# Paged decode steps moved between the steps of a stick-breaking attention sweep

## The reference

```python
def block(inp):                       # prompt, 128 queries at a time
    z = jnp.einsum('bqhd,bshd->bhqs', qi, kf) * Dh ** -0.5 + bias
    mask = kpos[None, :] < pi[:, None]
    l1mb = jnp.where(mask, jax.nn.log_sigmoid(-z), 0.0)
    after = lax.cumsum(l1mb, axis=3, reverse=True) - l1mb
    A = jnp.where(mask, jnp.exp(jax.nn.log_sigmoid(z) + after), 0.0)
    return jnp.einsum('bhqs,bshd->bqhd', A, vf)
```

## Time and profile before

| what | value |
|---|---|
| time, median of 3 runs | 1577.14 us (1576.19 to 1581.95) |
| the profiled execution | 1576.19 us, span 1574.2 us |
| PE busy | 1292.1 us (82% of the span) |
| DVE, ACT, POOL busy | 844.5, 485.1, 357.4 us |
| mean granted clock of PE | 0.897 |
| stage of the change | about 151 to 560 us of the span |

### The profile page before, as it was taken

How to read it: one execution, slowest core, us unless ns; L and a number is a source line. 1 busy time by engine, 2 the same in 40 slices (tenths; PEclk the granted TensorE clock), 3 DMA queues, 4 the chain that set the end, 5 groups by cost and what they waited for, 6 DMA issues and landing times. The chain is left out here.

```text
span 1574.2 us, 23116 instructions
## 1 busy us (share of the span) xinstructions
PE 1292.1 (82%) x7719; PEld 1082.3 (69%) x7719; DVE 844.5 (54%) x1198; ACT 485.1 (31%) x902; POOL 357.4 (23%) x235
## 2 busy tenths in 40 slices
PE   3549599799798855878969789499999998697997
PEld 2449467677576545878968789478787886365885
DVE  4434789889795613847668387244444443323221
ACT  5312345345355512141331413231313131222110
POOL 0027544343340002536334264000000000000000
PEclk7679789899898987999989999698999898798998
DMA  4536657477382505464444642285656541543320
GB/s 134 161 115 205 208 178 243 136 223 234 124 249 74 181 23 183 135 195 135 141 130 129 198 143 83 92 252 166 188 164 187 165 148 70 176 151 112 107 80 28
DMA packets 200420, 237.89 MB, mean 151 GB/s; under 512 B 13539, under 2 KB 122434, under 8 KB 200298
## 3 DMA queue, kind: packets, MB, share of 16 engines
q1 hardware_dynamic: 196338, 224.61, 46.2%
q0 software_dynamic: 3968, 11.87, 2.1%
HBM read 215.88 MB, written 20.64 MB: 150 GB/s over the span
## 5 line engine op out<-in xcount | busy, mean ns | idle before, releaser
L248 PE MATMUL bank<-xh,b_w_hi 128*128 128x344 f32 x480 | 167.0, 348 | 57.4 <-ACT b_mix L257 17.5
L1961 POOL TENSOR_TENSOR cp_keys<-cp_keys,cp_q 128x1024 f32<-128x1024 f32 x64 | 161.0, 2533 | 159.0 <-DMA cp_keys<-cache_sb_k 158.9
L1961 POOL TENSOR_TENSOR bp_keys<-bp_keys,bp_q 128x1024 f32<-128x1024 f32 x64 | 156.8, 2470 | 177.0 <-DMA bp_keys<-cache_sb_k 169.2
L248 PE MATMUL bank<-xl,b_w_hi 128*128 128x344 f32 x480 | 162.5, 339 | 0.0
L248 PE MATMUL bank<-xh,b_w_lo 128*128 128x344 f32 x480 | 162.4, 338 | 0.0
L248 PE MATMUL bank<-xh,d_w_hi 128*128 128x344 f32 x384 | 131.4, 342 | 24.2 <-DVE d_w_lo L231 16.5
L317 PE MATMUL bank<-xh,c_w_hi 128*128 128x344 f32 x384 | 130.3, 339 | 17.0 <-DVE c_w_lo L303 17.0
L248 PEld LDWEIGHTS bank<-xh,b_w_hi 128*128 128x128 f32 x480 | 98.6, 205 | 61.8 <-ACT b_w_hi L226 24.0
L317 PE MATMUL bank<-xl,c_w_hi 128*128 128x344 f32 x384 | 127.1, 331 | 0.0
L317 PE MATMUL bank<-xh,c_w_lo 128*128 128x344 f32 x384 | 126.7, 330 | 0.0
L248 PE MATMUL bank<-xl,d_w_hi 128*128 128x344 f32 x384 | 126.5, 329 | 0.0
(11 more groups left out here) (381 smaller groups left out, 2587.9 us busy)
## 6 DMA issues: line engine op xcount, KB each, us to landing
cp_keys<-cache_sb_k SPq DMA_DIRECT2D x128, 256.0 KB, 3.0
cp_values<-cache_sb_v SPq DMA_DIRECT2D x128, 256.0 KB, 3.0
bp_keys<-cache_sb_k SPq DMA_DIRECT2D x128, 256.0 KB, 3.1
dp_values<-cache_sb_v SPq DMA_DIRECT2D x128, 256.0 KB, 2.8
b_w_raw<-w_in SPq DMA_DIRECT2D x20, 512.0 KB, 4.0
c_w_raw<-w_in SPq DMA_DIRECT2D x16, 512.0 KB, 5.3
d_w_raw<-w_in SPq DMA_DIRECT2D x16, 512.0 KB, 5.1
o_mix<-mix SPq DMA_DIRECT2D x8, 1024.0 KB, 5.7
```

The lines of the kernel that those rows point to most:

```text
L248: last = self.nc.tensor.matmul(self.bank(j, c)[:, 0:self.width], w[:, s, k, :], x[:, k, c * self.width:(c + 1) * self.width], start=(k == ...
L1961: self.nc.gpsimd.tensor_tensor(self.keys[:, s], self.keys[:, s], q, ALU.mult).then_inc(self.scaled.sem, 1)
```

## The change

The paged parts are put at other steps. Taking and gathering the sum of the sample before goes to the very top of step 0 on both engines, and keeping it to the end of step 0. The page sums and the exponents go from step 2 to step 1, ACT's exponential from step 3 to step 2. The eight groups of paged weighings stood in steps 4 to 11 and now stand in steps 3 to 6 and 8 to 11.

```diff
-    GROUPS = (4, 5, 6, 7, 8, 9, 10, 11)
+    GROUPS = (3, 4, 5, 6, 8, 9, 10, 11)
...
@@ block.scalar
-                if u == 3 and i < GT:
+                if u == 2 and i < GT:
                     load_tables(nc, act, LN_EXP)
                     act.wait_ge(values.weighed.sem, values.weighed.at(i, 0))
                     keys.weights(act, i)
...
@@ block.vector
                 i, u = g // NU, g % NU
+                if u == 0 and i:
+                    values.take_partial(dve, i - 1)
                 if u == V_TURNED + 1:
...
                 if u == 0 and i:
-                    values.take_partial(dve, i - 1)
-                if u == 1 and i:
                     values.keep(dve, i - 1)
-                if u == 2 and i < GT:
+                if u == 1 and i < GT:
                     keys.exponents(dve, i)
...
@@ block.tensor
                 i, u = g // NU, g % NU
+                if u == 0 and i:
+                    values.gather(pe, i - 1)
                 if g < LAST:
                     scores(g)
                 if g in chunk_of:
                     stream.chunk(pe, *chunk_of[g][1:])
-                if u == 1 and i:
-                    values.gather(pe, i - 1)
-                if u == 2 and i < GT:
+                if u == 1 and i < GT:
                     if i:
                         pe.wait_ge(values.kept.sem, values.kept.at(i, 0))
                     keys.sum_pages(pe, i)
```

## The result

| | before | after |
|---|---|---|
| median (range, runs) | 1577.22 us (1576.19 to 1581.95, 4) | 1596.87 us (1591.54 to 1603.41, 4) |
| ratio after/before | | 1.012, 95% interval 1.0078 to 1.0164 |
| profiled execution, its span | 1576.19, 1574.2 us | 1599.24, 1597.2 us |
| stage of the change | 460.8 us | 474.3 us |
| mLSTM stage, two stages on | 405.5 us | 413.2 us |

The changed kernel is slower, and its median lies 0.9 us above the upper end of the range. The stage times are the distances between barriers; the stages not named moved by 1.2 us at most.

The account below looks back on a forecast made before the run. PE was taken as the bound (busy 89% of sweep 1), with stage changes entering the span one for one. Terms 3.2 + 4.4 + 3.0 + 6.4 - 3.0 - 3.0 + 1.0 = +12.0 us gave 1588 us, range 1576 to 1596.

Parts of the forecast that it names:

- boundary 0/1, wait, gather, clock: From sweep 0 to 1, PE waits 3.2 us for the masked copy ahead of the gather; low clock adds 3.2.
- boundary 1/2, wait, gather, clock: From sweep 1 to 2, PE waits 4.35 us for the masked copy ahead of the gather; low clock adds 3.2.
- gather's time, given back: Gather moves from step 1 to step 0 on PE and costs nothing net; page sums take its place.
- boundary 2/3, steps 11 to 2: From sweep 2 to 3, no chunk in step 0: PE starts 4.8 us later, partly an old wait; +3.0 us.
- steps 3 and 4 of sweeps 1 and 2: Exponents one step earlier free DVE ahead of the copy PE awaits in step 4: -1.5 us each, -3.0 in all.
- weighings, values: Four paged weighings one step earlier: waits for values of 0.85 and 2.71 us go; -3.0 us in sum.
- end of sweep 3: PE waits for the copy between its last weighing and the gather: +1.0 us, bounds 0 and 1.0.
- The clock: After idling at the two boundaries with a chunk, PE runs about 6.4 us at half clock: +3.2 us each, +6.4.
- the clock stays up: Rival: 3 to 4 us of idling does not lower PE's clock at two boundaries; +5.6 us, 1582 us, chance 0.15.
- It is worse: Rival: clock down as long as in sweep 3 at each boundary, POOL products hit moved scans; 1596 us, chance 0.08.
- the scan goes first: Rival: step 3's scan keeps the port ahead of POOL, saving 9.3 us in two sweeps; 1570 us, chance 0.05.
- the broken burst: Rival: POOL's four products break up, scan enters after two, saving 4.7 us in sweeps 1 and 2; 1579, chance 0.10.

Follow-up runs that it names:

- second trace: Changed kernel run again with nothing altered: 1592.64 us, ratio 1.0094; for the kernel before, likewise run again unaltered: 1578.82 us, ratio 1.0004.
- short products: GpSimd's key products over 64 of 512 columns, as a test only: 1565.87 us in the changed kernel, 1547.25 us in the kernel before.
- old groups: Changed kernel with the eight groups of paged weighings back at steps 4 to 11: 1599.44 us, ratio 1.0132.
- the kernel with the later store: Changed kernel with the gather at the end of step 0 and GpSimd's store of the gated half three key pairs later: 1562.47 us, ratio 0.9879.
- the kernel before with the later store: Kernel before with only GpSimd's store of the gated half put three key pairs later (pair 8 for 5): 1569.45 us, ratio 0.9936.

## Why the prediction was right and wrong

The direction, the cause and its place were right: a copy queued on DVE behind the softplus holds PE at every boundary. The gather alone at the top brings the loss, and the gather at the end of the step removes it. The size was off. The measured terms, from the length of the steps (the start of one step's scores to the next), both traces against the first trace of the kernel before; against its second trace the sum is 3.6 us more:

| term | forecast | first trace | second trace |
|---|---|---|---|
| boundary 0/1, wait, gather, clock | 3.2 + 3.2 | +8.4 | +8.5 |
| boundary 1/2, wait, gather, clock | 4.4 + 3.2 | +11.9 | +13.0 |
| gather's time, given back (page sums took its place in step 1, and left step 2) | 0 net | -1.7 | -1.7 |
| boundary 2/3, steps 11 to 2 | +3.0 | +0.1 | +0.4 |
| steps 3 and 4 of sweeps 1 and 2 | -3.0 | -4.7 | -4.7 |
| weighings, values | -3.0 | -5.1 | -3.0 |
| end of sweep 3 | +1.0 | +4.8 | +3.2 |
| sweep 0 and its start | 0 | -0.2 | -2.5 |
| sum | +12.0 | +13.5 | +13.1 |

**The step that failed is the size of the waits at boundaries 0/1 and 1/2.** They were forecast at 3.2 + 4.4 us and measured at 5.2 + 9.4 (second trace 6.0 + 9.6). Two things were missed.

The first is when PE arrives. The prediction took its arrival from before and only moved the copy. But that arrival held a wait for values ahead of the last weighing: 1.52 us at 0/1, and 1.0 us at 1/2. Both went with the change, apart from 0.66 us at 0/1 in the second trace. The prediction called 0.85 and 2.71 us the largest such waits in reach and passed over the 1.52 us in its own row. With short products, where POOL cannot disturb DVE for long, the wait is 4.72 us at every boundary.

The second is the queue ahead of the copy. At 1/2 the prediction asked whether the copy could be shut out by POOL, and answered with an operation that reads PSUM. That was right: at 272.03 the copy took its 0.68 us inside a product that ran from 271.79 to 274.31. It did not ask the same of the multiplications ahead of it, which read two tiles in SBUF. They lost 4.2 us, as the moved weighings brought the key products forward; the old groups and the short products both took that away.

**The clock** was priced about right, at 3.2 + 3.2 us. What the steps grew by is new idle time, the gather and the clock. PE's work in steps 11 and 0 is 14.3 us before and 15.3 us with the gather at the full clock. In the changed kernel it is 19.0 and 17.8 us (second trace 17.7 and 18.6), so the low clock costs 3.8 + 2.5 = 6.3 us (2.4 + 3.4 = 5.8). The idle time grew by 3.7 and 8.4 us, the waits less the values' waits that went, and the gather's 1.0 us each makes up the rest of +8.4 and +11.9. The rival in which the clock stays up is refuted at all three boundaries. The rival "It is worse" has the number of the first result, 1596, but not its terms: the clock was down for 10.2 us at each of the two boundaries, as in sweep 3 of before, and cost 6.3 us and not 10; and POOL's products hit the multiplications ahead of the copy, while the moved scans of the exponents took 0.2 us each.

**Boundary 2/3** was forecast at +3.0 and cost nothing. The kernel before already stood 3.33 us there and already ran at the low clock. In steps 11 to 2 PE's idle time grew only from 4.1 to 5.7 us, since most of the old wait went, and its work fell from 22.9 us (22.3 in the second trace of before) to 21.4 (21.7). The low clock there lasted 10.2 and 6.8 us before and 6.8 us in both traces after. **The end of sweep 3** was forecast at +1.0 and cost 3 to 5. The copy stood behind both multiplications of the last step (562.12 to 563.39), so the wait was 2.26 us and not 0.68, and with the low clock the transposes and the weighing behind it took nearly twice as long. The prediction applied the clock to two boundaries and left out the end.

**The savings** were real and too low: the kernel with the gather at the step's end shows them undisturbed. The waits for values nearly went, as forecast, and in sweep 3 steps 8 to 10 gained 4.7 us (4.3 in the second trace). Steps 3 and 4 took 2.0 to 2.8 us less a sweep, where 1.5 were taken; against the mean of both traces of before it is 2.0. The old groups keep this gain and the gather alone does not have it, so it belongs to the page sums, the exponents and ACT's exponential, which moved together.

**The scans** stayed shut out, 11.62 us. The Trainium skill (SBUF — State Buffer, section "SBUF: two separate sides") has the pair of ports locked for one instruction. The traces agree with that nearly everywhere: each of the two multiplications above waited for one product though the products stood back to back, and in the kernel with the later store a scan beside one product of 2.45 us took 2.52. In the mLSTM stage of before, POOL runs four products in a row, and a scan gets in behind each:

```profile
706.41 9.38 POOL L1961 TENSOR_TENSOR bp_keys<-bp_keys,bp_q 128x1024 f32<-128x1024 f32 x4 [2.60 <-DMA mix<-b_mix]
...
708.78 2.43 DVE L2009 TENSOR_TENSOR_SCAN bp_page_soft<-ones,bp_page_L 128x32 f32<-128x32 f32 x1
```

The exception is the first scan of step 3, which waited for all four; the second one then took 1.2 us:

```profile
297.37 10.54 DVE L567 TENSOR_TENSOR_SCAN c_left<-c_keep,ones 128x512 f32<-128x512 f32 x1
```

It is so in all ten traces in which these four products run in a row behind the store, in both sweeps. Why this scan, which starts 0.1 us ahead of the first product, gets no turn between them is open. The rival in which the scan goes first is refuted. What the rival of the broken burst described, 4.7 us saved in each of two sweeps, did not come with the change, but it did when the store was moved: steps 3 and 4 take 23.0 us in place of 28.0 in the kernel before with the later store.

In all: the stage was forecast at +12.0 and took +13.1 to +13.5 against the same trace, and +15 by both pairs. That it came so near is partly luck. In the first trace the two boundaries and the end of sweep 3 cost 10.1 us more than forecast, and the other terms came out 8.6 us lower. In the first profiled execution some 8 us more lay in the mLSTM stage and did not come again. They are no term of the sum; whether they carried the median over the end of the range the single runs do not show. By the first set of runs the forecast is 9 us low, by the second 4.6.

## What to carry to other kernels

A wait placed at the head of the bounding engine's step must be priced from where that engine will arrive after the change, and from everything queued ahead of the releaser, each instruction asked on its own whether it can be shut out. Where a change removes waits ahead of a new one, the saving is partly paid back there. Where the reader stands decides: the stage took 474 us with the gather at the top of the step, 467.2 behind the chunk and 451.6 at the step's end. Measure each move alone before they are taken together.

## What the runs showed of the hardware

- A DVE instruction with two inputs in SBUF waits out the POOL product that it meets, and only that one, also when products stand back to back: multiplications of 2.77 and 2.82 us in place of 0.7 beside two products (5.3 us), a softplus step of 2.56 in place of 0.42 us, scans of 2.43 us beside four in a row. One case is otherwise in every trace that has it: the first scan of step 3, begun 0.1 us ahead of four products (9.3 us), took 10.5 us. Why is open.
- A copy that reads PSUM and one SBUF tile is not held by a product: 0.68 us inside one of 2.52 us.
- A small gather of 8 matmuls takes 1.87 us at the 1.2 GHz level and 1.05 at 2.4.
- Behind waits of 5.2 to 9.6 us at a boundary the low clock cost 2.4 to 3.8 us; it also came behind waits of 2.26 us (end of sweep 3) and 2.04 us (first boundary, gather at the step's end).
- Filling PE's wait at the second boundary with small matmuls (64 by 128), 0.96 us of idle time left, put the fall of the clock off until behind the gather and cut its price there to 1.5 us, but did not prevent it. Why it fell all the same is open.
- A stage that no edit touches (mLSTM) took 404.7 to 416.6 us over the traces, more than most terms of this case. One trace does not carry a term of that size.
